# A hybrid diffusion layer on one core: projections moved between the first head's scores, a second order for the output projection, a shorter router chain

## The reference

```python
h = rmsnorm(x) * (1 + scale1) + shift1                 # modulation from c, by w_ada
u = h @ w_in                                           # split: conv (2x512) | q (384) | kv (256) | rotary key (64)
conv = silu(layernorm(depthwise31(a * sigmoid(g))))    # 512 wide
q = rmsnorm(u_q) @ w_uq                                # 4 heads of 128 + 64 rotary
k_nope, v = split(ckv_keys @ w_ukv)                    # keys: 128 cached + own tokens; per head 128 + 128
att = softmax((q_nope k_nope + q_rope k_rope) / sqrt(192)) @ v
out = concat(conv, att) @ w_out
x = x + gate1 * rmsnorm(out)
h2 = rmsnorm(x) * (1 + scale2) + shift2
# router: best of 4 groups, then the two best of its 8 experts (32 experts in all)
y = sum_e gate_e * (silu(h2 @ w_gate[e]) * (h2 @ w_up[e])) @ w_down[e]
x = x + gate2 * rmsnorm(y)
```

## Time and profile before

| what | us |
|---|---|
| median of three runs | 702.93 |
| the profiled execution | 703.74 |
| its span, first to last instruction | 701.9 |
| PE busy | 583.8 (83%) |
| DVE busy | 264.5 (38%) |
| ACT busy | 150.9 (21%) |
| POOL busy | 81.2 (12%) |

### The profile page before, as it was taken

One profiled execution on the slowest core, in us unless ns is written; L12 is line 12 of the kernel. 1 busy time (PEld: TensorE's weight loads), 2 busy tenths in 40 slices (PEclk: granted clock), 3 DMA queues, 4 the chain that ended last, 5 costly groups with the idle time before them and its releaser, 6 DMA issues.

```text
span 701.9 us, 9338 instructions
## 1 busy us (share of the span) xinstructions
PE 583.8 (83%) x3734; PEld 339.9 (48%) x3734; DVE 264.5 (38%) x455; ACT 150.9 (21%) x301; POOL 81.2 (12%) x100
## 2 busy tenths in 40 slices
PE   0899999999999889989999474899899898777720
PEld 0666666555555445544455362455455454434300
DVE  2315999999743244402232460011011010100017
ACT  3320000112425344422223310101101100110125
POOL 6000002200000000001111026021121121110001
PEclk9999999999999989999999867999999999999965
DMA  9999943000007810045213951689999999999859
GB/s 339 350 393 404 405 164 140 14 0 1 1 1 276 317 74 1 1 143 217 120 61 127 420 222 26 240 348 423 421 426 423 421 424 423 423 425 424 357 212 270
DMA packets 47635, 173.33 MB, mean 247 GB/s; under 512 B 5738, under 2 KB 12235, under 8 KB 35290
## 3 DMA queue, kind: packets, MB, share of 16 engines
q1 hardware_dynamic: 39856, 158.47, 56.2%
q0 software_dynamic: 6448, 12.54, 5.6%
q10 hardware_dynamic: 1274, 1.52, 0.6%
HBM read 162.79 MB, written 17.06 MB: 256 GB/s over the span
## 4 chain that ended last, share of the span: by engine, by line
PE 61%; DMA 16%; SPq 9%; DVE 4%; ACT 3%; another core or an unknown queue 2%; issue 2%; DVEq 1%; ACTq 1%; POOLq 0%
PE ps L1365 14%; PE ps L1631 10%; PE ps L1696 8%; SPq L480 8%; DMA arena<-in_w_up 5%; PE ps L1712 5%; DMA arena<-in_w_down 5%; PE ps L1366 4%; PE ps L1429 3%; DMA arena<-in_w_ada 3%; PE ps L1383 3%; PE ps L1599 3%; PE ps L1567 3%; PE ps L1370 2%
## 5 line engine op out<-in xcount | busy, mean ns | idle before, releaser
L1696 PE MATMUL ps<-arena 128*64 128x256 f32 x992 | 112.7, 384 | 19.9 <-ACT arena L944 11.2
L1365 PE MATMUL ps<-arena 128*128 128x512 f32 x216 | 111.1, 596 | 0.7 <-issue 0.6
L1696 PEld LDWEIGHTS ps<-arena 128*64 128x64 f32 x992 | 72.8, 138 | 62.9 <-issue 12.8
L1074 DVE SCALAR_TENSOR_TENSOR arena<-arena 128x655 f32<-128x655 f32 x116 | 95.9, 906 | 0.4 <-issue 0.2
L1712 PE MATMUL ps<-arena 128*64 128x512 f32 x256 | 61.9, 627 | 18.4 <-ACT arena L944 12.9
L1370 PE MATMUL ps<-cst,arena 128*128 128x128 f32 (+2 forms) x349 | 52.8, 297 | 24.7 <-DVE arena L1013 16.1
L1631 PE MATMUL ps<-arena 128*128 128x512 f32 x160 | 69.2, 593 | 0.9 <-ACT arena L896 0.9
L1366 PEld LDWEIGHTS ps<-arena 128*128 128x128 f32 x216 | 41.0, 190 | 51.6 <-issue 51.6
L1370 PEld LDWEIGHTS ps<-cst,arena 128*128 128x128 f32 (+2 forms) x349 | 43.9, 179 | 37.3 <-issue 30.2
L1311 DVE TENSOR_TENSOR arena<-arena,ps 128x256 f32<-128x256 f32 x16 | 6.7, 421 | 116.8 <-ACT arena L950 116.8
L1326 DVE COPY arena<-ps 128x1024 f32<-128x1024 f32 x15 | 18.4, 1224 | 84.2 <-PE ps L1712 84.2
(11 more groups left out here) (269 smaller groups left out, 604.5 us busy)
## 6 DMA issues: line engine op xcount, KB each, us to landing
arena<-in_w_up SPq DMA_DIRECT2D x15, 2048.0 KB, 28.9
arena<-in_w_down SPq DMA_DIRECT2D x15, 2048.0 KB, 27.5
arena<-in_w_gate SPq DMA_DIRECT2D x14, 2048.0 KB, 27.0
arena<-in_w_ada SPq DMA_DIRECT2D x12, 2048.0 KB, 13.0
arena<-y_d SPq DMA_DIRECT2D x10, 512.0 KB, 7.2
arena<-in_w_out SPq DMA_DIRECT2D x1, 4096.0 KB, 12.6
arena<-ada_d SPq DMA_DIRECT2D x8, 512.0 KB, 8.0
x<-in_w_gate SPq DMA_DIRECT2D x2, 2048.0 KB, 25.9
```

What stands on the lines that cost most here:

```text
L1074: ins = dve.scalar_tensor_tensor(dst, src, w, dst, ALU.mult, ALU.add)
L1365: mm(pp(name)[:, 0:TS], lhs(k), rhs_s(k), start=k == 0, stop=k == steps - 1)
L1696: last = mm(ps[a:a + ROWS, s, n * FE:(n + 1) * FE], src[:, k, a:a + ROWS], w[:, j, k * FE:(k + 1) * FE], start=k == 0, stop=k == KD - 1)
```

## The change

Four groups of edits.

1. Keys and values are no longer made ahead of attention. `head_groups(0)` now holds them: `k0`, `k1`, scores 0 and 1, `v0`, `v1`, scores 2 and 3, `v2`, `v3`, `S4`, `v4`, `v5`, `k2`, `k3`, then the turns. ACT's copies move into its head loop. `proj_act` is gone; PE waits for `k{h}` to be read. SP loads `w_out` after `k3` instead of `v5`. In every head the prompt's scores come ahead of the output of the head before.
2. The output projection takes the convolution's pieces first. Block 0's are made ahead of `O3`. `POST` has a new order. `P4` is made half by half, and its norm is worked by halves; POOL's addition of `b2` is gone: DVE multiplies by `a2` early, and one instruction scales and adds.
3. Router logits: `rt` is made as two sums of four products, in output partitions 0 to 35 and 64 to 99; ACT copies both, and `rl` adds them by a product with a 0/1 matrix. `number` is made by ACT; `pos` is read from PSUM; `round_ids` is shorter; the softmax differences come after the places.
4. The first pair's rows are copied in two halves, and its gate products start after the first.

```diff
-POST = ["P0", "P1", "P2", "ht0", "P3", "rt0", "ht1", "P4", "rl0", "rt1", "ht2", "ht3", "rl1", "rt2", "rl2", "rt3",
-        "rl3", "ht4", "rt4", "rl4"]
-BETWEEN = (("rl0", "rt1", "ht2"), ("ht3", "rl1", "rt2", "rl2", "rt3", "rl3"))
+POST = ["P0", "P1", "ht0", "P2", "rt0", "ht1", "P3", "rl0", "rt1", "ht2", "P4", "rl1", "rt2", "rl2", "ht3", "rt3", "rl3",
+        "ht4", "rt4", "rl4"]
+BETWEEN = (("rl1", "rt2"), ("rl2", "ht3", "rt3", "rl3"))
...
-            landed(sp, "v5")
+            landed(sp, "k3")
...
             act.dma_start(state_krope[0, 0], sto[:, KVL:]).then_inc(state_out, 16)
-            for h in range(H):
-                name = f"k{h}"
-                landed(act, name)
-                act.activation(kn[:, h, TP + PAST:], pp(name)[:, 0:TS], ACT.Copy)
-                free(act.activation(kn[:, h, 0:TP + PAST], pp(name)[:, 512:512 + TP + PAST], ACT.Copy), name)
-            for t in range(KT):
-                name = f"v{t}"
-                landed(act, name)
-                free(act.activation(vv[:, t, :], pp(name)[:, 0:512], ACT.Copy), name)
-            act.drain().then_inc(proj_act, 1)
             act.wait_ge(state_out, 32)
...
-                    free(act.activation(lg, pp(name)[0:G + E, 0:P], ACT.Identity, bias=rbias[:]), name)
+                    act.activation(lg[0:G + E], pp(name)[0:G + E, 0:P], ACT.Identity, bias=rbias[:])
+                    free(act.activation(lg[DR:], pp(name)[DR:DR + G + E, 0:P], ACT.Copy), name)
...
+                if name == f"P{NT - 1}":
+                    half = h2T[1].rearrange("p k t -> p (k t)")[:, 0:512]
+                    landed(act, "rt1")
+                    act.wait_ge(p_half, 1)
+                    act.activation(half, pp(name)[:, 0:512], ACT.Square, accum_out=stat[:, 0, b:b + 1]).then_inc(pss, 1)
                     landed(act, name)
+                    act.wait_ge(pss, NT)
+                    act.activation(half, pp(name)[:, 512:], ACT.Square, accum_out=stat[:, 3, b:b + 1]).then_inc(pss, 1)
+                    act.wait_ge(rest_ready, 1)
+                    act.wait_ge(pss, NT + 1)
+                    act.activation(stat[:, 5, b:b + 1], stat[:, 3, b:b + 1], ACT.Sqrt, bias=stat[:, 1, b:b + 1], scale=1.0 / D).then_inc(psd, 1)
+                    for other in BETWEEN[0]:
+                        read_out(other)
...
+                    for other in BETWEEN[1]:
+                        read_out(other)
+                    act.wait_ge(h2_ready, NT)
+                    act.dma_start(h2_d[b * P:(b + 1) * P, :], h2[:, b % 2, :]).then_inc(h2_st[b % 2], 16)
...
+            for c, hit in enumerate(chosen):
+                act.wait_ge(oh_ready, c + 1)
+                for b in range(NT):
+                    act.activation(number[:, c, b, 0, :], hit[:, b, :], ACT.Copy, scale=cst[:, C_HI + c * NT + b:C_HI + c * NT + b + 1])
+                act.activation(number[:, c, :, 1, :], hit, ACT.Copy, scale=cst[:, C_LO:C_LO + 1]).then_inc(number_ready, 1)
...
+            def second_norm(b):
+                v = min(b, 1)
+                if b >= 2:
+                    dve.wait_ge(h2_st[b % 2], 16 * (b // 2))
+                    landed(dve, f"ht{b - 2}")
+                dve.tensor_tensor(h2[:, b % 2, :], x[:, b, :], a2[:, v, :], ALU.mult)
...
+                dve.scalar_tensor_tensor(h2[:, b % 2, :], h2[:, b % 2, :], stat[:, 7, b:b + 1], b2[:, v, :], ALU.mult, ALU.add).then_inc(h2_ready, 1)
...
             for h in range(H + 1):
+                if h == 0:
+                    keys(0)
+                    keys(1)
+                    pe.wait_ge(proj_dve, 1)
                 if h < H:
+                    emptied(pe, f"k{h}")
                     scores(h, (0, 1))
                 if h:
                     turned((h - 1) * NT + 2)
                     turned((h - 1) * NT + 3)
+                else:
+                    values(0)
+                    values(1)
                 if h < H:
                     scores(h, (2, 3))
+                if h == 0:
+                    values(2)
+                    values(3)
+                if h < H:
+                    prompt_scores(h)
+                if h == H:
+                    pe.wait_ge(wo_in, 16)
+                    begin(pe, "P0")
+                    pe.wait_ge(mixc_ready, CM)
+                    output(0, [(k, half) for k in range(CM) for half in range(2)])
                 if h:
                     head_output(h - 1)
+                else:
+                    values(4)
+                    values(5)
+                    keys(2)
+                    keys(3)
...
+                    for k in range(KD // 2):
+                        for at in range(2):
+                            last = mm(pp(name)[DR * at:DR * at + G + E, 0:P], wr[:, at * KD // 2 + k, :], h2T[b % 2][:, at * KD // 2 + k, :],
+                                      start=k == 0, stop=k == KD // 2 - 1)
...
-                    last = turn(pp(name)[:, 0:G + E], lg, G + E)
+                    last = mm(pp(name)[:, 0:G + E], lg, dup[0:DR + G + E, 0:G + E], start=True, stop=True)
```

More of the change, by code:

```diff
@@ L151, in pe_groups @@
             names.append("lnv")
-    names += ["state"] + [f"k{h}" for h in range(H)] + [f"v{t}" for t in range(KT)]
+    names.append("state")
     for h in range(H + 1):
         names += head_groups(h)
-    return names + POST + ["pos", "table0", "table1"]
+    return names + POST[1:] + ["pos", "table0", "table1"]
 def hybrid_layer(nc, i, outs):
@@ L1159, in _ @@
             dve.wait_ge(b2_in, 32)
[L1160 to L1171, removed]
+            dve.memset(lg[DR // 2:DR], 0.0).then_inc(lg_zero, 1)
@@ L1192, in _ @@
             Lg, Le = L[:, :, 0:G], L[:, :, G:]
-            em, eq, oh1, oh2, pos = (wide(n) for n in range(5))
+            em, eq, oh1, oh2 = (wide(n) for n in range(4))
             goh, geq, pen, m1, m2, top = (narrow(5, G, 0), narrow(5, G, 1), narrow(5, G, 2), narrow(5, 1, 16), narrow(5, 1, 20), narrow(5, 1, 24))
@@ L1544, in _, with keys, values @@
             pe.wait_ge(wukv_in, 16)
-            for h in range(H):
+            def keys(h):
                 both(f"k{h}", lambda k: wukv[:, k, h * (DN + DV):h * (DN + DV) + DN],
                      lambda k: ck[:, k, TP + PAST:], lambda k: ck[:, k, 0:TP + PAST], KM, TP + PAST)
-            for t in range(KT):
+            def values(t):
                 name = f"v{t}"
@@ L1600, in head_output, with output @@
                 done(mm(g[:, 512:512 + TP], vv[:, 0, h * DV:(h + 1) * DV], pTp, start=True, stop=True), name)
+            def output(b, steps):
+                name = f"P{b}"
+                for n, (k, half) in enumerate(steps):
+                    last = mm(pp(name)[:, half * 512:(half + 1) * 512], mixT[:, k, b * P:(b + 1) * P],
+                              wo[:, k, half * 512:(half + 1) * 512], start=k == 0, stop=k == KD - 1)
+                    if b == NT - 1 and n == KD - 1:
+                        last.then_inc(p_half, 1)
+                return last
             for h in range(H + 1):
+                if h == 0:
+                    keys(0)
+                    keys(1)
+                    pe.wait_ge(proj_dve, 1)
                 if h < H:
+                    emptied(pe, f"k{h}")
                     scores(h, (0, 1))
@@ L1626, in _ @@
                             emptied(pe, f"O{h}")
-                    for k in (*range(CM, KD), *range(CM)):
-                        if b == 0 and k == 0:
-                            pe.wait_ge(mixc_ready, CM)
-                        for half in range(2):
-                            last = mm(pp(name)[:, half * 512:(half + 1) * 512], mixT[:, k, b * P:(b + 1) * P],
-                                      wo[:, k, half * 512:(half + 1) * 512], start=k == CM, stop=k == CM - 1)
+                        last = output(0, [(k, half) for k in range(CM, KD) for half in range(2)])
+                    else:
+                        begin(pe, name)
+                        if b < NT - 1:
+                            last = output(b, [(k, half) for k in range(KD) for half in range(2)])
+                        else:
+                            last = output(b, [(k, half) for half in range(2) for k in range(KD)])
                 elif kind == "ht":
-                    if b < NT - 1:
-                        pe.wait_ge(h2_ready, b + 1)
-                    else:
-                        pe.wait_ge(h2_last, 1)
+                    begin(pe, name)
+                    pe.wait_ge(h2_ready, b + 1)
                     for k in range(KD):
```

176 lines of the change are left out of this document (111 added, 65 removed).

## The result

The changed kernel takes 706.79 us (median of 10 runs, 705.96 to 709.01), the kernel before 704.35 (10 runs on the same chip, 700.96 to 705.72): ratio 1.0045, 95% interval 1.0027 to 1.0062. It is slower, by 2.4 us in the medians and 3 us by the ratio; the forecast was 0.3 us faster. The forecast time, 702.7 us, was counted from the median of the first three runs, 702.93; over ten runs that median is 704.35, so 1.4 of the 4.1 us between 702.7 and 706.79 have nothing to do with the change. The profiled execution took 706.36 us with a span of 704.6 (703.74 and 701.9 before); the mean granted clock went from 0.950 to 0.945.

The account below looks back on a forecast made before the run. Experts wait for weights, their end a fixed time behind the first pair, so the sum follows the chain of waits before it: 4.8 - 1.56 + 1.5 - 4.2 - 0.7 + 0.4 - 0.5 = -0.3, giving 702.7 us; range 697 to 708.

Parts of the forecast that it names:

- Keys and values moved, +4.8: Before head 1: ACT's wait for the second state store holds k0's copy, so PE idles and its clock slows; +4.8 us.
- the spread works: Rival for keys and values: store lands early or ACT isn't held; idle time fills, -6.6 instead of +4.8, 691.3 us; chance 0.13.
- The prompt's scores earlier, -1.56: Attention heads: PE's 0.52 us wait for DVE's division of S4 is covered in three heads; -1.56 us.
- The convolution's products first, +1.5: Last turn to P4's end: half of P0 covers a wait, but P4 waits for P3 to be scaled; +1.5 us.
- rt in two halves, 1.05: Router logits: two column groups run beside each other, so an rt takes about 1.05 us instead of 1.94.
- The rival that they don't run side by side: Rival for rt: its halves run one after the other; +3.3 us, 706.0 us in all; chance 0.12.
- After P4, -4.2: P4's end to the router's first instruction: 11.65 us instead of 15.87, held by the queue of read-outs; -4.2 us.
- Router, -0.7: Router: pos read when it lands, fewer number instructions and PSUM copies, shorter round_ids; -0.7 us.
- Gather, +0.4: First gather: issued 26 us after P4, it meets the loads still moving for under a microsecond; +0.4 us.
- Half copy, -0.5: First pair: gate products start 1.0 us earlier but ACT's stop covers them; ACT is ready 0.5 earlier; -0.5 us.
- ACT's stop: Entry of the experts: two ACT stops of 13.25 and 3.51 us that the profile can't name; the sum leaves them unchanged.
- the rivals that it grows or shrinks: ACT's stop at the experts' entry: longer, 706.2 or 716 us, chance 0.09; shorter, 699.2 us, chance 0.05.

Follow-up runs that it names:

- Experiment 1: Changed kernel with ACT's wait for the two state stores moved from ahead of its head loop to behind it: 686.18 us, ratio 0.9883 to the kernel before.
- experiment 2: Kernel before with only ACT's wait for the two state stores moved ahead of its copies of keys and values: 699.87 us, ratio 1.0078 to the kernel before.
- experiment 3: Changed kernel with keys and values made and copied ahead of attention again, all other edits kept: 691.36 us, ratio 0.9951 to the kernel before.
- experiment 5: Changed kernel with rt whole again: one column group, one ACT copy, a transpose back: 698.23 us, ratio 1.0057 to the kernel before.
- Experiment 4: Changed kernel with products nobody reads filling PE's idle times behind P4: 697.29 us, ratio 1.0032 to the kernel before.
- experiment 6: Changed kernel with load 9 issued only after the rows of pairs 0 and 1 are gathered: 696.59 us, ratio 1.0035 to the kernel before.
- experiment 7: Changed kernel with unread products behind P4 and load 9 issued behind the gather: 694.95 us, ratio 1.0011 to the kernel before.
- experiment 8: Changed kernel with ACT's store wait behind the head loop, unread products behind P4 and load 9 late: 683.20 us, ratio 0.9865 to the kernel before.

## Why the prediction was wrong, step by step

- **Keys and values moved, +4.8:** right. Counted from k0, ACT was to stand until 14.2 us and stood until 14.17; PE was to go on at 15.3 and went on at 15.14; the slow clock followed. Head 1 started 41.73 us after k0 against 37.3 at full clock before: +4.4. Experiments 1 and 2 show the cause from both sides. The rival "the spread works" fell for this kernel, and was nearly right in size for the one with the wait moved: -8.8 against -6.6 - 1.56 = -8.2.
- **The prompt's scores earlier, -1.56:** right in kind, -2.1 together with a little else; experiment 3 has -1.8 with k and v in their old place, and -2.2 without its longer time at the low clock (the first scores of head 1 take 4.30 us there, 3.87 before).
- **The convolution's products first, +1.5:** +1.5. The wait for P3 is there, with the releaser named.
- **rt in two halves, 1.05:** 1.07 us at full clock. The rival that they don't run side by side fell. The Trainium skill, TensorEngine Tiling (Array Packing), Key Properties, says that a change of tiling mode drains TensorE; in the rows of rt0 and of ht1 behind it (351.43 and 352.43) the next product starts with the end of the last, and no time for a drain is seen.
- **After P4, -4.2:** the step that failed. It came to -1.3, outside its own bounds of -4.7 and -2.0. All its durations were taken at 2.4 GHz, and the clock fell to 1.2 at about 391.9, ahead of ht4. The argument even had the material: PE's work in the first 7.4 us behind P4 was nearly halved, from 6.30 to 3.60 us, while the waits for ACT stayed, and the prediction itself had priced a fall of the clock behind two other pauses of PE. Of this loss the halves of rt made 1.7 us; with the rest of the change alone (experiment 5, 5.26 us) the clock stayed up. Experiment 4 puts the fall at 2.1 of the 2.9 us missed. The other 0.8 us is there at full clock too (12.43 us against 11.65): ht4 starts 7.55 us after P4 instead of 7.2, and from there to the router it is 4.9 us instead of 4.45; what they come from was not tested.
- **Router, -0.7:** -0.65. **Gather, +0.4:** +0.6, but the reasoning was too easy. (The 2.3 us in which the gather before moves its rows don't stand in the earlier trace rows; in the trace they move from 413.5 on, for about 2.7 us.) With the read-outs as quick as forecast the gather would have gone out 2 us sooner into the same loads, as in experiment 4 (7.72 us to the turns, +3.2). Had the failed step been right, this one would have failed in its place, and the sum of both would have been near what it is: in experiment 4 it is 34.0 us from P4 to the turns, in the changed kernel 33.5.
- **Half copy, -0.5:** ACT's copy for the extra round came 19.15 us after the turns instead of 19.5, so -0.35 of it was there. The extra round's gate products behind it took 9.50 us in the chain against 8.72, which makes the stretch +0.4; the half copy by itself was not tried.
- **ACT's stop:** 12.99 + 3.91 us idle before, 16.50 + 0.43 after. Two stops became one with the same sum; the rivals that it grows or shrinks fell.

Of the 3.0 us between the sum forecast (-0.3) and measured (+2.7), the stretch behind P4 is 2.9. The others are off by -1.6 (start, k0 to the last turn) and +1.7 (gather, load 12, end and router) and cancel within 0.1 by luck; the -0.7 at the start and the +0.5 at the end lie where nothing was forecast to change.

## What to carry to other kernels

When work moves past a wait, the wait has to move too: ask of every wait left behind what is now queued behind it, for here one line of ACT turned a gain of 8.8 us in its stretch into a loss of 2.3. When products on a chain with waits are made shorter, price the chain at the lower clock as well, since PE's share of busy time falls with them. And a gather that is released sooner gained nothing while the transfers ahead of it were still in the queues. Moving one of them behind it in the same edit shortened the stretch to the turned rows in experiments 6 to 8; that it shortens the whole is not proven by the times.

## What the runs showed that was not expected

- ACT's stop at the entry of the experts belongs to the chip or the launch, not to the kernel. In the two kernels of the result ACT stands there behind its first copy, and the profile names only `remote` as what ended it (changed kernel, timeline of ACT):

```profile
436.34 0.38 ACT L983 ACTIVATE arena<-ps 128x256 f32<-128x256 f32 x1 [16.50 <-remote]
```

In all eight kernels of the experiments, on two chips, the same instruction waits 7.2 to 8.4 us for PE's gate products, and the stretch to load 12 takes 30.4 to 31.8 us instead of 41. That is about the 10 us by which the kernel before differs (704.35 against 694.35 and 693.55). Experiment 1 (timeline of ACT):

```profile
418.97 0.38 ACT L984 ACTIVATE arena<-ps 128x256 f32<-128x256 f32 x1 [7.94 <-PE ps L1800]
```

- P4's end to the turns of the gathered rows took 33.5, 33.7, 34.0, 33.4 and 33.9 us in the changed kernel and in experiments 1, 4, 5 and 3, whatever the read-outs took. In the kernel before, whose gather went out when the loads behind P4 were done, it was 34.9. With load 9 behind the gather it was 32.7, 32.4 and 30.9 (experiments 6, 7 and 8). The reading is that the loads behind P4 are a volume, and the gather's rows come when they have gone through; experiments 6 and 8 fit it, the 6.10 us of experiment 7 only in part.
- 16 products in two groups of 36 columns take 1.07 us, in one group 1.91 to 1.94 at the same clock.
- The second of two small stores, issued behind three expert loads, lands 9.3 to 10.2 us after its issue in all ten profiles; in experiment 1 nobody waits for it.
